# A hybrid DeltaNet and attention layer: the last two levels of the triangular inverse, formed once for all heads

## The reference

```python
lower = jnp.where(tri_strict, jnp.einsum('bhnid,bhnjd->bhnij', kbc, kc) * decay, 0.0)
t_mat = lax.linalg.triangular_solve(eye + lower, jnp.broadcast_to(eye, lower.shape),
                                    left_side=True, lower=True, unit_diagonal=True)
u = jnp.einsum('bhnij,bhnje->bhnie', t_mat, vbc)
...
out = jnp.einsum('bsd,de->bse', merged, w_out)
return x + rms_norm(out, norm_post_w)
```

## Time and profile before

| | |
|---|---|
| median of 3 runs | 357.48 us (357.46 to 357.59) |
| profiled execution | 357.55 us, span 355.8 us |
| PE busy | 347.6 us (98%) |
| PE weight loads | 318.4 us (89%), beside the products |
| DVE busy | 270.0 us (76%) |
| ACT busy | 218.8 us (62%) |
| POOL busy | 58.7 us (16%) |
| weight thirds of the head stage (L1395) | 3 x 440 products, 40% of the chain that ended last |

### The profile page before, as it was taken

The page is one execution under the profiler, slowest core; times in us unless marked ns, Lnnn a source line. Parts: engine busy times, 40 slices in busy tenths (PEclk is TensorE's granted clock), DMA queues, the critical chain, the costliest instruction groups (busy, mean ns, idle before and its releaser), DMA issues.

```text
span 355.8 us, 6674 instructions
## 1 busy us (share of the span) xinstructions
PE 347.6 (98%) x2387; PEld 318.4 (89%) x2387; DVE 270.0 (76%) x551; ACT 218.8 (62%) x483; POOL 58.7 (16%) x114
## 2 busy tenths in 40 slices
PE   7999999999999999999999999999999999999993
PEld 5889998888899999999999999999998888888882
DVE  3869897599997868978788797878977656566744
ACT  5877894542457667686867766777676544425421
POOL 1534436500050000301103020030301101000011
PEclk9999999999999999999999999999999999999999
DMA  8667948793698485446745565465534735766423
GB/s 264 178 193 194 334 158 270 198 329 119 167 257 228 121 214 141 121 122 164 188 120 128 145 178 147 120 164 145 165 121 138 247 118 172 254 226 236 124 113 118
DMA packets 76206, 63.48 MB, mean 178 GB/s; under 512 B 4724, under 2 KB 62478, under 8 KB 76174
## 3 DMA queue, kind: packets, MB, share of 16 engines
q1 hardware_dynamic: 73838, 59.37, 57.3%
q0 software_dynamic: 1152, 3.30, 3.1%
q10 hardware_dynamic: 1184, 0.39, 0.5%
HBM read 61.46 MB, written 1.59 MB: 177 GB/s over the span
## 4 chain that ended last, share of the span: by engine, by line
PE 84%; DVE 8%; DMA 3%; issue 2%; ACT 1%; POOL 0%; DVEq 0%; SPq 0%; ACTq 0%; POOLq 0%
PE banks L1395 40%; PE banks L1450 15%; PE banks L1657 6%; PE banks L1413 6%; DVE w_lo L919 3%; DVE sub L1061 2%; DMA xin<-in_x_dram 1%; DMA raw<-in_w_in_dram 1%; DMA sub<-m_blocks 1%; PE banks L1545 1%; PE banks L1523 1%; PE banks L1562 1%; PE banks L1551 1%; PE banks L1380 1%; DVE sub L1063 1%
## 5 line engine op out<-in xcount | busy, mean ns | idle before, releaser
L919 DVE TENSOR_TENSOR w_lo<-raw,w_hi 128x1024 fp32r<-128x1024 f32 x102 | 123.8, 1220 | 42.3 <-ACT w_hi L670 41.6
L670 ACT CAST w_hi<-raw 128x1024 fp32r<-128x1024 f32 x103 | 107.2, 1047 | 30.0 <-PE banks L1450 12.3
L1395 PE MATMUL banks<-h_hi,w_hi 128*128 128x256 f32 x440 | 64.0, 288 | 0.2 <-DVE acc L989 0.2
L1395 PE MATMUL banks<-h_lo,w_hi 128*128 128x256 f32 x440 | 59.4, 277 | 0.0
L1395 PE MATMUL banks<-h_hi,w_lo 128*128 128x256 f32 x440 | 59.3, 277 | 0.0
L1395 PEld LDWEIGHTS banks<-h_hi,w_hi 128*128 128x128 f32 x440 | 55.2, 189 | 0.7 <-DVE acc L989 0.3
L1395 PEld LDWEIGHTS banks<-h_hi,w_lo 128*128 128x128 f32 x440 | 54.2, 188 | 0.0
L1395 PEld LDWEIGHTS banks<-h_lo,w_hi 128*128 128x128 f32 x440 | 54.2, 188 | 0.0
L989 DVE SCALAR_TENSOR_TENSOR acc<-banks,vec,acc 128x255 f32<-128x255 f32 (+2 forms) x72 | 34.5, 480 | 3.7 <-ACT acc L790 1.5
L616 POOL TENSOR_TENSOR so<-so,rnq 128x2 f32<-128x2 f32 x8 | 2.0, 251 | 162.8 <-ACT junk L857 162.8
L790 ACT ACTIVATE acc<-banks,vec 128x256 f32<-128x256 f32 x16 | 7.6, 473 | 17.4 <-PE banks L1395 17.4
(11 more groups left out here) (258 smaller groups left out, 607.6 us busy)
## 6 DMA issues: line engine op xcount, KB each, us to landing
raw<-in_w_in_dram SPq DMA_DIRECT2D x80, 512.0 KB, 4.9
raw<-in_w_branch_dram SPq DMA_DIRECT2D x16, 512.0 KB, 4.7
raw<-in_w_out_dram SPq DMA_DIRECT2D x8, 512.0 KB, 4.2
xin<-in_x_dram SPq DMA_DIRECT2D x2, 512.0 KB, 3.8
th_E<-g_rows POOLq DMA_DIRECT2D x2, 512.0 KB, 7.2
bias<-bias_rows POOLq DMA_DIRECT2D x1, 1024.0 KB, 7.5
raw<-in_x_dram SPq DMA_DIRECT2D x2, 512.0 KB, 3.7
out_dram<-xin SPq DMA_DIRECT2D x4, 256.0 KB, 2.0
```

The lines of the kernel that those rows point to most:

```text
L670: nc.scalar.copy(w_hi[:, t % SLOTS, :], raw[:, t % SLOTS, :]).then_inc(s_hi, 1)
L919: v.tensor_tensor(w_lo[:, t % SLOTS, cols], raw[:, t % SLOTS, cols], w_hi[:, t % SLOTS, cols].bitcast(F32), ALU.subtract).then_inc(s_lo, 1)
L1395: last = mm(ps, w, r, start=part == 0 and k == 0, stop=part == 2 and k == KT - 1)
```

## The change

The head-by-head `stage_u` and `compact` go. In their place stands `inverse(S)` on PE, ACT and DVE, which does both levels for all heads: the first level at S = 96 to 100 and the second in two halves of four heads at S = 102 to 106 and 120 to 124, with transposes of the diagonal blocks at S = 100 and 107. The first level is packed: of each head only the 32x32 blocks that take part stand in a 128x64 operand (`s1_all`, `m1_all`, `xs_all`, `m2_all`), so that a product has 64 weight columns and 64 moving columns, eight for each of its two steps. The operands are laid out by DMAs: GpSimd four for `s1_all`, four for `m1_all` ahead of the four for `T_all`; ACT four for `m2_t` at S = 91; GpSimd clears the buffers first. The second level keeps full-size products. One copy now moves the results of four or eight heads. `U_all` (in `la_all`'s place) holds all heads' transposed inverses, and `lac` all heads' blocks in one copy.

```diff
-U0, W0, UW_STRIDE = 99, 114, 18
+W0, W_STRIDE = 114, 18
+L1X, L1D = 96, 99
+L2X, L2D = (102, 120), (105, 123)
...
-        lac = sb("lac", [P, 2, 2, P])
+        lac = sb("lac", [P, HEADS, P])
...
-        u2, xl, oo, on = [two(0), two(256)], two(512), two(768), two(1024)
+        oo, on = two(768), two(1024)
...
+        U_all = la_all
+
+        def packed(flat, heads):
+
+            return flat.rearrange("p (h n) -> p h n", h=heads)
+
+        bottom, turned = sub[:, 512:1024], sub[:, 1536:2048]
+        s1_all, m1_all, m2_t, m2_all = (packed(a, HEADS) for a in (junk[:], sub[:, 0:512], bottom, turned))
+        xs_all, xl = packed(sub[:, 2048:2560], HEADS), packed(sub[:, 0:512], 4)
...
+            pool.wait_ge(s_ksq, 2 * HEADS)
+            pool.memset(junk[:], 0.0).then_inc(s_y_zero, 1)
+            pool.tensor_copy(lac[:].rearrange("p h (c x) -> p (h c) x", c=NC),
+                             la_all[:, :, :, HALF:].rearrange("p h c x -> p (h c) x")).then_inc(s_lac, 1)
+            pool.wait_ge(s_y_zero, 1)
+            for b in range(2):
+                for c in range(NC):
+                    lane = HALF * b + BLK * c
+                    pool.dma_start(s1_all[lane:lane + BLK, :, BLK * b:BLK * b + BLK],
+                                   la_all[HALF * b:HALF * b + BLK, :, c, HALF * b + BLK:HALF * b + HALF]
+                                   ).then_inc(s_l1_in, 16)
+            pool.wait_ge(s_lac, 1)
+            pool.wait_ge(s_l1_in, 64)
+            pool.memset(U_all.rearrange("p h c n -> p (h c n)"), 0.0).then_inc(s_y_zero, 1)
             pool.wait_ge(s_sub, 2 * STEPS)
             for a in range(2):
                 pool.dma_start(bass.AP(t_blocks.tensor, BLK * a, [[BLK * BLK, HALF], [2 * BLK, BLK // 2], [1, BLK]]),
                                t0[HALF * a:HALF * a + HALF]).then_inc(s_T_out, 16)
+            pool.memset(sub[:, 0:1024], 0.0).then_inc(s_y_zero, 1)
+            pool.memset(sub[:, 2048:2560], 0.0).then_inc(s_y_zero, 1)
+            pool.wait_ge(s_y_zero, 4)
             pool.wait_ge(s_T_out, 32)
+            for b in range(2):
+                for c in range(NC):
+                    lane = HALF * b + BLK * c
+                    pool.dma_start(m1_all[lane:lane + BLK, :, BLK * c:BLK * c + BLK],
+                                   t_blocks[c::NC, 2 * b].rearrange("a r n -> r a n")).then_inc(s_l1_in, 16)
...
-            def compact(g):
-
-                if g >= 2:
-                    pool.wait_ge(s_x_p, 2 * g - 2)
-                la = la_all[:, g]
-                pool.tensor_copy(lac[:, g % 2, 0, :].rearrange("p (b c x) -> p b c x", b=2, c=NC),
-                                 la.rearrange("p c (b x) -> p b c x", b=2)[:, :, :, BLK:HALF]).then_inc(s_lac, 1)
-                pool.tensor_copy(lac[:, g % 2, 1, :].rearrange("p (c x) -> p c x", c=NC), la[:, :, HALF:]).then_inc(s_lac, 1)
-                pool.wait_ge(s_lac, 2 * g + 2)
-
-            compact(0)
-            compact(1)
...
+            def inverse(S):
+
+                if S == L1X - 5:
+                    sa.wait_ge(s_T_out, 32)
+                    sa.wait_ge(s_y_zero, 4)
+                    for b in range(2):
+                        for c in range(NC):
+                            lane = HALF * b + BLK * c
+                            sa.dma_start(m2_t[lane:lane + BLK, :, BLK * c:BLK * c + BLK],
+                                         t_blocks[c::NC, 2 * b + 1].rearrange("a r n -> r a n")).then_inc(s_m2_in, 16)
+                elif S == L1X + 1:
+                    sa.wait_ge(s_inv_x, 1)
+                    found = bD[BLK:HALF, :].rearrange("p (h c n) -> p h c n", h=HEADS, c=NC)
+                    for c in range(NC):
+                        lane = HALF + BLK * c
+                        nc.scalar.copy(xs_all[lane:lane + BLK, :, BLK:HALF], found[:, :, c, :]).then_inc(s_inv_c, 1)
+                elif S == L1D + 1:
+                    sa.wait_ge(s_inv_d, 1)
+                    found = bD[BLK:HALF, :].rearrange("p (h c n) -> p (h c) n", h=HEADS, c=NC)
+                    nc.scalar.copy(U_all[HALF:HALF + BLK, :, :, HALF + BLK:].rearrange("p h c n -> p (h c) n"),
+                                   found).then_inc(s_inv_u, 1)
+                for half in range(2):
+                    found = bD[HALF:, :].rearrange("p (h c n) -> p h c n", h=4, c=NC)[:, :, 1, :]
+                    if S == L2X[half] + 1:
+                        sa.wait_ge(s_inv_x, half + 2)
+                        nc.scalar.copy(xl[HALF:, :, HALF:], found).then_inc(s_inv_c, 1)
+                    elif S == L2D[half] + 1:
+                        sa.wait_ge(s_inv_d, half + 2)
+                        nc.scalar.copy(U_all[0:HALF, 4 * half:4 * half + 4, 1, HALF:], found).then_inc(s_inv_u, 1)
...
-            def stage_u(g, s):
...
+            def inverse(S):
+
+                def diagonal(blocks):
+
+                    for i in blocks:
+                        part = slice(BLK * i, BLK * i + BLK)
+                        v.transpose(U_all[part, :, :, part].rearrange("p h c n -> p (h c) n"),
+                                    T_all[part, :, :, part].rearrange("p h c n -> p (h c) n")).then_inc(s_inv_t, 1)
+
+                if S == L1X:
+                    ve.wait_ge(s_m2_in, 64)
+                    v.transpose(turned, bottom).then_inc(s_inv_t, 1)
+                elif S == L1X + 1:
+                    ve.wait_ge(s_inv_x, 1)
+                    found = bD[0:BLK, :].rearrange("p (h c n) -> p h c n", h=HEADS, c=NC)
                     for c in range(NC):
+                        v.tensor_copy(xs_all[BLK * c:BLK * c + BLK, :, 0:BLK], found[:, :, c, :]).then_inc(s_inv_c, 1)
+                elif S == L1D + 1:
+                    ve.wait_ge(s_inv_d, 1)
+                    corner = U_all[0:BLK, :, :, BLK:HALF].rearrange("p h c n -> p (h c) n")
+                    v.tensor_copy(corner, bD[0:BLK, :].rearrange("p (h c n) -> p (h c) n", h=HEADS, c=NC)).then_inc(s_inv_u, 1)
+                    ve.wait_ge(s_inv_u, 2)
+                    ve.wait_ge(s_T_in, 16 * NBLK)
+                    v.transpose(T_all[BLK:HALF, :, :, 0:BLK].rearrange("p h c n -> p (h c) n"), corner).then_inc(s_inv_t, 1)
+                    diagonal((2, 3))
+                elif S == L2D[0] + 2:
+                    diagonal((0, 1))
+                for half in range(2):
+                    found = bD[0:HALF, :].rearrange("p (h c n) -> p h c n", h=4, c=NC)[:, :, 0, :]
+                    if S == L2X[half] + 1:
+                        ve.wait_ge(s_inv_x, half + 2)
+                        v.tensor_copy(xl[HALF:, :, 0:HALF], found).then_inc(s_inv_c, 1)
+                    elif S == L2D[half] + 1:
+                        ve.wait_ge(s_inv_d, half + 2)
+                        v.tensor_copy(U_all[0:HALF, 4 * half:4 * half + 4, 0, HALF:], found).then_inc(s_inv_u, 1)
...
-            def stage_u(g, s):
...
+            def inverse(S):
+
+                if S == L1X:
+                    pe.wait_ge(s_l1_in, 128)
+                    pe.wait_ge(s_gate_b, 6)
+                    for h in range(HEADS):
+                        last = mm(bD[0:HALF, HALF * h:HALF * h + HALF], s1_all[:, h, :], m1_all[:, h, :], start=True, stop=True)
+                    last.then_inc(s_inv_x, 1)
+                elif S == L1D:
+                    pe.wait_ge(s_inv_c, 4)
+                    pe.wait_ge(s_inv_t, 1)
+                    for h in range(HEADS):
+                        last = mm(bD[0:HALF, HALF * h:HALF * h + HALF], xs_all[:, h, :], m2_all[:, h, :], start=True, stop=True)
+                    last.then_inc(s_inv_d, 1)
+                for half in range(2):
+                    if S == L2X[half]:
+                        pe.wait_ge(s_lac, 1)
+                        if half:
+                            pe.wait_ge(s_inv_u, 4)
+                        else:
+                            pe.wait_ge(s_inv_u, 2)
+                            pe.wait_ge(s_inv_t, 2)
+                        for i in range(4):
+                            last = mm(bD[:, P * i:P * i + P], lac[:, 4 * half + i, :], T_all[:, 4 * half + i, :, 0:HALF], start=True, stop=True)
+                        last.then_inc(s_inv_x, 1)
+                    elif S == L2D[half]:
+                        pe.wait_ge(s_inv_c, 2 * half + 6)
+                        pe.wait_ge(s_inv_t, 4)
+                        for i in range(4):
+                            last = mm(bD[:, P * i:P * i + P], xl[:, i, :], U_all[:, 4 * half + i, :, HALF:], start=True, stop=True)
+                        last.then_inc(s_inv_d, 1)
...
+                    pe.wait_ge(s_inv_u, 2 * (g // 4) + 4)
+                    pe.wait_ge(s_inv_t, 6)
```

More of the change, by code:

```diff
@@ L278, in build @@
         s_cst = sem("s_cst")
-        s_d_p = sem("s_d_p")
         s_f = sem("s_f")
@@ L394, in build @@
         s_zero = sem("s_zero")
+        s_y_zero = sem("s_y_zero")
+        s_l1_in = sem("s_l1_in")
+        s_m2_in = sem("s_m2_in")
+        s_inv_x = sem("s_inv_x")
+        s_inv_c = sem("s_inv_c")
```

(41 more changed lines are left out.)

41 lines of the change are left out of this document (removed).

## The result

The changed kernel takes 359.28 us (median of 6 runs, 359.15 to 360.42) against 357.57 (357.46 to 357.59) for the kernel before in the same rounds: a ratio of 1.0054, 95% interval 1.0041 to 1.0066. The change makes the kernel slower by 0.4 to 0.5%, where I had forecast 0.2% faster.

The account below looks back on a forecast made before the run. PE's own work was taken to set the end. From 357.55 us, -1.3 for PE's balance, +0.1 for `m1_all` and +0.5 for the slot 111 wait gave 356.85 (356.8 on the median's scale), range 355.4 to 358.6.

Parts of the forecast that it names:

- GpSimd and the queues before slot 96: GpSimd and DMA work before slot 96: clear, `lac` copy and `s1_all` transfers free in GpSimd's idle time; `m1_all` charged 0.1 us.
- The balance of PE: PE work over all heads: -7.25 us removed, +3.55 second level, +2.4 first level, net -1.3 us, between -1.95 and -0.1.
- What comes: Work added on PE: 16 full-size second-level products, 3.55 us, and 32 records of packed first-level products, 2.4 us.
- What goes: Four `stage_u` products a head leave PE, three at 0.222 us and a lone one at 0.24: 7.25 us for eight heads.
- The small products: Packed first-level products on PE, 64 by 64 columns: 0.075 us a record, bounds 0.055 and 0.11, 2.4 us for 32.
- Rival C: Packed products on PE cost as much as full ones; gain only 0.15 to 0.5 us, total 357.1 to 357.5; chance 0.12.
- The wait at slot 111: PE at slot 111 needs the last tap of tile 35 from DVE; zero margin, wait 0 to 2 us, taken as 0.5.
- Rival D: DVE bounds the first head; PE's wait at slot 111 is 1.0 to 2.0 us, total 357.0 to 358.0; chance 0.12.
- `m1_all`: Four transfers due for slot 96: issued 102.2 to 104.8 us, landing 3.5 to 4.7 us later; 0.1 us charged.
- rival E: Last `m1_all` transfer lands late for slot 96 because DMA queues are full; at 7.1 us PE waits 2.4, 358.6; chance 0.14.
- ACT's issues: Four `m2_t` DMA issues on ACT from slot 91: about 0.5 us each; `act` about 0.1 us later, still ahead of PE.
- The clear of `sub`: GpSimd clears 1536 columns behind the `t_blocks` stores, some 1.4 us, inside its 3.15 us wait for them: costs nothing.

Follow-up runs that it names:

- after_again: The changed kernel unaltered, measured in a second set of rounds: 359.56 us against 357.75 for the kernel before, ratio 1.0044.
- act_copy: Changed kernel with diagonal transposes of blocks 0 and 1 five slots later and the `lac` copy on ACT at S = 73: 357.06 us against 357.72.
- copy_twice: Changed kernel with GpSimd's copy of `lac` issued twice, one behind the other: 360.01 us against 357.67 for the kernel before, ratio 1.0059.
- before_pool_copy: Kernel before, with only GpSimd's clear and two half-size copies added at the same place: 358.35 us, ratio 1.0012.
- copy_late: Changed kernel with only the `lac` copy moved behind the landing of the `s1_all` blocks, some 9 us later: 358.73 us, ratio 1.0028.
- after: The changed kernel itself, first set of rounds: 359.28 us against 357.57 for the kernel before, ratio 1.0054; its profiled execution took 360.42 us.
- pool_early: Changed kernel with GpSimd's clear of `junk` and copy of `lac` moved ahead of its wait for the stored blocks: 357.93 us, ratio 1.0005.
- copy_pieces: Changed kernel with late diagonal transposes and the `lac` copy cut into eight of 128 columns, each waiting for the one before: 357.40 us, ratio 1.0001.
- diag_late: pool_early with DVE's transposes of diagonal blocks 0 and 1 moved from S = 107 to S = 112: 357.18 us against 357.72, ratio 0.9985.
- gap_copy: diag_late with GpSimd's clear and copy still earlier, ahead of its value norms, at about 62 us: 358.91 us, ratio 1.0038.

## Why the prediction was wrong, point by point

**The step that failed** is in "GpSimd and the queues before slot 96": "so clearing `junk`, copying all of `lac` and the four `s1_all` transfers lie in free time". It was free time of GpSimd, and I asked nothing else: the term was put at nothing. The copy runs beside DVE's substitution, and it stopped DVE for 1.6 us. In the kernel before, DVE is busy 25.71 of the 26.63 us from this step to the end of the substitution's loop (70.67 to 97.30): 0.92 us free, which is less than the hold. After it, in the windows of after_again (stretch, its length, DVE busy with its count, granted clock, DMA share, GB/s):

```profile
70.90:99.50 28.60, 27.71 (x49) 1.00 0.66 200
```

The held time counts as busy in this row, and the idle time is what it was, 0.9 us: DVE made up next to nothing. The lag reaches PE: 1.45 to 1.6 us up to slot 90, and 2.47 with two copies. Four runs carry it: take the copy off GpSimd and PE is on time at slot 95 (act_copy), make it twice and both the hold and PE's loss grow by 0.8 to 0.9 us (copy_twice), give the old kernel the copies and its DVE steps are held (before_pool_copy), move the copy and the held instruction moves with it (copy_late). With 1.5 us for that term the forecast of 356.85 becomes 358.4.

The Trainium skill has the rule, "SBUF — State Buffer", section "Who interferes with whom": a DVE instruction with two SBUF inputs contends with a GpSimd instruction that reads SBUF, not with one that only writes it. I had not weighed it. The traces agree at each point: every held instruction is a TENSOR_TENSOR with both inputs in SBUF, the TENSOR_REDUCE rows between keep their length (0.17), and the clear holds nothing. By it a rival in which DVE stands still for the length of the copy belonged in the prediction. For DVE's 2-port modes, not for this case, the same section of the Trainium skill says that the engine that comes second is blocked for the whole instruction of the other. The step that ends within 0.03 us of the copy's end would fit that; the hold of 1.63 us, longer than the copy's record of 1.05, is not explained by it.

**The balance of PE** (predicted -1.3 us). act_copy, which has almost no waits, gives it directly: -0.01 us at slot 95 and -0.69 at the end, so -0.7. What comes is nearly as predicted: 2.55 us for the packed products (predicted 2.4) and 0.78 to 0.86 for the groups of four full ones (predicted 0.89), 5.9 in all against 5.95. What goes was mis-sized: two heads of after are 20.81 us apart, as the same weight third of the timeline of PE shows,

```profile
158.86 1.17 PE L1444 MATMUL banks<-h_hi,w_hi 128*128 128x256 f32 x8
...
179.67 1.17 PE L1444 MATMUL banks<-h_hi,w_hi 128*128 128x256 f32 x8
```

where the kernel before has 21.63. That is 0.82 a head, 6.6 us for eight and not 7.25. The four slots give 0.17, 0.20, 0.21 and 0.24: only the lone product, the last, reached its price from the earlier trace rows; one that shares a slot with others gives back up to 0.05 us less than its step in the chain.

**The small products**: 0.068 us a record at first cost, 0.060 for more of the same, against my 0.075 and the bounds 0.055 and 0.11; with the slower weight thirds behind the groups it is 0.080. Rival C falls. The two rules of the Trainium skill, "TensorE: Matmul & The Clock Gate", that I had set beside it gave 81 ns at 128 columns ("Back-to-back issue gap") and 53 ns at 64 ("LDWEIGHTS (loading the stationary operand)"); the row at 64 columns gives 68, between the two.

**The wait at slot 111** (predicted 0.5, zero margin by my count): 0.65 us in after and pool_early, 0.43 in after_again, and 0.75 us in the median when it is taken away. The step was right. The terms in it were only about right: the four diagonal transposes stand as pairs in after,

```profile
118.93 1.44 DVE L1187 STREAM_TRANSPOSE xin<-T_all 32x512 f32<-32x512 f32 x2
```

0.72 each, where I had put 0.63. Rival D was this wait at 1 to 2 us; it stayed below that.

**`m1_all`** (predicted 0.1): 0 in after, 0.43 in after_again, 0.4 in copy_late, 0 in pool_early. Its transfers landed 3.2 to 4.5 us after their issue in after, near; the weight loads' 7.1 us never showed, so rival E falls. The wait stands in the two executions in which the slowest took 5.1 us, and in none in which it took 4.5 or less, copy_twice with its later DVE among them: it is rival E's mechanism at a small size. Why those two were slower isn't shown.

**ACT's issues** took 1.95 to 3.10 us for four (predicted 2.0), and no wait of PE leads to them. **The clear of `sub`** in front of the four loads took 1.04 + 0.60 us and was followed by 2.03 us of waiting for the stores, as I had said: GpSimd's clears were free, only its copy was not.

**The sum** for after_again, +2.3 us: -0.7 for PE's work, +1.5 for the copy (slot 95), +0.33 that was there ahead of it, +0.43 and 0.06 at slot 96, 0.43 for the wait at slot 111, and 0.25 more, in pieces of less than 0.1, in the slots 100 to 110, which I can't assign (all measured against act_copy). The forecast's -0.7 had the first, at nearly twice its size, and the waits of slots 96 and 111. Had the one failed step been right, it would have come out near 357.9, as pool_early did: no change rather than faster. The mis-sized balance is the second, smaller error.

**What stays open.** Why the held step begins 0.7 us before the copy's recorded start (starts on GpSimd are rough); what the +0.4 us at slot 90 in pool_early and copy_pieces is (diag_late, with pool_early's order of work up to there, has 0.02); why a product taken out of a shared slot gives 0.17 to 0.21 us; and what delayed the blocks in gap_copy.

## What to carry to other kernels

An idle engine is not free time: before work is put on GpSimd, look at what DVE does in the same microseconds, and where DVE's own slack is used up, put copies on ACT, or in small pieces, or where DVE idles anyway (that worked in pool_early and not in gap_copy); clears may stay. A margin of zero in a count of several microseconds is a wait to plan for: move what nobody needs yet (here five slots) rather than hope for the gaps. Removed work is best priced by the period of a steady stage and not by the duration of one instruction, since it gave back 10% less here than its records promised.

## What the runs showed of the hardware that was not expected

- A GpSimd copy of 128x1024 FP32, 1.05 us alone, held a DVE multiplication of 12 columns for 1.63 us; beside longer two-input instructions it held 0.81 to 0.87 us (a 128x512 step, a `w_lo` in copy_twice, and the `w_lo` pairs that it met in pool_early and gap_copy); two copies of 512 columns held 0.65 us, eight of 128 columns 0.3 us. The hold is mutual: the copy's own record grew to 1.58 to 1.82 us, and the eight pieces took 4.39, where eight times 0.30 would be 2.4 (an estimate from the 128x128 copies of the kernel before).
- A GpSimd clear of 128x512 FP32 (0.55 us) beside a two-input DVE instruction held nothing: `w_lo` kept its 1.22 us in act_copy. Neither did one of 128x2048 (1.82 us, at 79.21 in after_again), beside which the steps of 240 and 128 columns kept their 0.40 and 0.29 us. A copy of 128x1024 on ACT (1.05 us) added nothing to the time.
- A 128-row FP32 product of 64 weight columns and 64 moving columns costs 0.060 to 0.068 us a record, at 1.00 granted clock, against 0.11 for the full form.
- A DVE transpose of 32x512 takes 0.70 to 0.72 us, where the line through smaller shapes led to 0.73 and the expected overlap of neighbours did not come.
- PE's lag ahead of the copy was 1.54 us in one execution of the changed kernel and 0.33 in another, a difference of 1.2 us, nearly the size of the effect studied here: a ledger by slot has to be read from where the edit begins.
